# A hybrid decoder trunk on one NeuronCore: operand places in SBUF, the order of four stretches, and a latent projection in three passes

## What is computed

```python
def reference(x, p, positions, ...):
    for i in range(DEPTH):                       # DEPTH = 2
        proj = rms_norm(x, attn_norm[i]) @ w_in[i]     # stick-breaking, latent, window and block heads
        # A: z = q k^T / 8; log_beta = log_sigmoid(z); log_keep = log_sigmoid(-z), strictly causal
        #    tail = reversed cumulative sum of shifted log_keep; w = exp(log_beta + tail); o_a = w v
        # B: c_q, c_kv = rms_norm of 192 and 128 of proj's 352 latent columns, 32 more are the rotary key
        #    q, k, v from c_q @ mla_w_uq and c_kv @ mla_w_ukv; causal softmax
        # C: window of 128, 2 kv heads, sinks; D: block attention (one block here): causal softmax
        x = x + rms_norm(groups) @ w_o[i]              # the four groups side by side
        u = causal_depthwise_conv(rms_norm(x, ffn_norm[i]) @ w_up[i])     # 1024 -> 2 x 2816, width 3
        x = x + (silu(u[..., :2816]) * u[..., 2816:]) @ w_down[i]
        x = x + (p[i] @ ple_proj[i]) * sigmoid(x @ ple_gate[i])
    return x
```

## Time and profile before

| what | value |
|---|---|
| median of three runs | 682.27 us (681.94 to 682.47) |
| the profiled execution's own time | 682.88 us, its span 681.1 us |
| TensorE busy | 669.8 us, 98% of the span |
| VectorE, ScalarE, GpSimd busy | 438.0, 420.8 and 391.7 us |
| mean granted TensorE clock | 1.0 |
| DMA | 115.18 MB, 168 GB/s of HBM over the span |

### The profile page before, as it was taken

How to read it: one execution, slowest core, us unless ns; L and a number is a source line. 1 busy time by engine, 2 the same in 40 slices (tenths; PEclk the granted TensorE clock), 3 DMA queues, 4 the chain that set the end, 5 groups by cost and what they waited for, 6 DMA issues and landing times.

```text
span 681.1 us, 9499 instructions
## 1 busy us (share of the span) xinstructions
PE 669.8 (98%) x3772; PEld 578.2 (85%) x3772; DVE 438.0 (64%) x619; ACT 420.8 (62%) x627; POOL 391.7 (58%) x214
## 2 busy tenths in 40 slices
PE   7999999999999999999999999999999999999997
PEld 5988988888888888888889889888888888888885
DVE  6876877739898985003378587866589898920033
ACT  5559775667777775334464797646777767643342
POOL 5423200278888887987830232104888888889871
PEclk9999999999999999999999999999999999999999
DMA  9951132575565555553396422144555555555411
GB/s 321 384 199 63 63 109 78 185 242 187 186 191 192 194 192 197 201 193 104 105 305 210 136 83 92 63 146 164 187 188 191 192 192 194 192 204 193 155 31 63
DMA packets 74445, 115.18 MB, mean 169 GB/s; under 512 B 2336, under 2 KB 58272, under 8 KB 74144
## 3 DMA queue, kind: packets, MB, share of 16 engines
q1 hardware_dynamic: 73248, 111.75, 49.1%
q10 hardware_dynamic: 1152, 2.81, 1.1%
HBM read 113.51 MB, written 1.05 MB: 168 GB/s over the span
## 4 chain that ended last, share of the span: by engine, by line
PE 92%; ACT 3%; DVE 3%; DMA 1%; issue 0%; SPq 0%; ACTq 0%; DVEq 0%
PE ps L1356 23%; PE ps L924 13%; PE ps L926 13%; PE ps L925 13%; PE ps L1358 12%; PE ps L938 2%; PE ps L1011 2%; PE ps L1048 2%; PE ps L976 1%; PE ps L1031 1%; PE ps L1002 1%; DMA raw<-w_in 1%; PE ps L1041 1%; DVE wl L1547 1%; ACT pr L601 1%; PE ps L1133 1%
## 5 line engine op out<-in xcount | busy, mean ns | idle before, releaser
L453 POOL TENSOR_TENSOR wl<-raw,wh 128x2048 fp32r<-128x2048 f32 (+1 forms) x72 | 323.9, 4503 | 81.9 <-ACT wh L570 81.9
L1356 PE MATMUL ps<-hT_hl,wh 128*128 128x512 f32 x688 | 239.6, 392 | 0.0
L570 ACT ACTIVATE wh<-raw 128x2048 fp32r<-128x2048 f32 (+1 forms) x102 | 186.0, 1828 | 75.5 <-PE ps L926 69.4
L1358 PE MATMUL ps<-hT_hl,wl 128*128 128x256 f32 x688 | 193.7, 282 | 0.0
L1356 PEld LDWEIGHTS ps<-hT_hl,wh 128*128 128x128 f32 x688 | 129.2, 188 | 28.7
L1358 PEld LDWEIGHTS ps<-hT_hl,wl 128*128 128x128 f32 x688 | 129.4, 188 | 0.0
L440 POOL TENSOR_SCALAR st<-st 128x2 f32<-128x2 f32 (+3 forms) x26 | 8.1, 310 | 148.2 <-ACT lat L629 75.1
L924 PE MATMUL ps<-wh,hT_hl 128*128 128x512 f32 (+1 forms) x220 | 80.6, 366 | 0.0
L926 PE MATMUL ps<-wh,hT_hl 128*128 128x512 f32 (+1 forms) x220 | 79.1, 359 | 0.0
L925 PE MATMUL ps<-wl,hT_hl 128*128 128x512 f32 (+1 forms) x220 | 78.9, 358 | 0.0
L1831 DVE TENSOR_TENSOR x<-x,ps 128x512 f32<-128x512 f32 x16 | 10.8, 687 | 100.1 <-PE ps L926 98.0
(11 more groups left out here) (296 smaller groups left out, 1164.7 us busy)
## 6 DMA issues: line engine op xcount, KB each, us to landing
raw<-w_up SPq DMA_DIRECT2D x44, 1024.0 KB, 5.1
raw<-w_down SPq DMA_DIRECT2D x22, 1024.0 KB, 4.9
raw<-w_in SPq DMA_DIRECT2D x16, 1024.0 KB, 8.7
raw<-w_o SPq DMA_DIRECT2D x6, 1024.0 KB, 4.9
raw<-ple_gate SPq DMA_DIRECT2D x6, 1024.0 KB, 4.9
raw<-w_in SPq DMA_DIRECT2D x4, 704.0 KB, 5.3
ng<-norm_gains ACTq DMA_DIRECT2D x2, 1024.0 KB, 6.1
raw<-w_o SPq DMA_DIRECT2D x4, 512.0 KB, 3.5
```

Source lines behind the costliest of these rows:

```text
L453: pool.tensor_tensor(wl[:, slot, 0:n], raw[:, slot, 0:n], w_high(u)[:, 0:n].bitcast(F32), ALU.subtract).then_inc(ffn_l_made, 1)
L570: act.activation(w_high(u)[:, c:n], raw[:, slot, c:n], ACT.Copy).then_inc(h_made, 1)
L1356: pe.matmul(both, high[:, c], hU_all[:, k].rearrange("p a n -> p (a n)"), start=k == 0, stop=False, skip_group_check=True)
L1358: mm = pe.matmul(o, wl[:, slot, c], hU_h[:, k, :], start=False, stop=k == KT - 1, skip_group_check=True)
```

## The change

The changes are these. The slots of `wh` become three tensors with small tables between them, so that they start 9,216 bytes apart (8,320 before), and most other tensors are put in another order; the FFN still reads `wh` 128 bytes further on. `M_MLA_B` in layer 0 and `M_MLA_A`'s second token tile in layer 1 are multiplied in three passes, with new high and low parts (`latent_high`, `latent_low`, `latent_A`). The row of roots is made by two transposes. `high(3)` and `low(3)` stand ahead of the scaling and the sums of the latents. The softplus sums stand ahead of `mla_T(1)`, with `low(8)`, `high(8)` and the low parts `sp_low` moved in the same way. The transposes of the probabilities of groups 1 and 2 stand ahead of an output quarter. The first two `x_T` of layer 1 stand inside layer 0's last gate products.

```diff
-        wh = sb("wh", [P, RING, SLOT + UP_AT], F32R)
-        sb("wh_edge", [P, 256 - RING * UP_AT])
+        wh0 = sb("wh0", [P, SLOT + UP_AT], F32R)
+        rope_c = sb("rope_c", [P, TT, HD])
+        ident_b = sb("ident_b", [P, P], BF16)
+        inv_freq = sb("inv_freq", [P, HD // 2])
+        wh1 = sb("wh1", [P, SLOT + UP_AT], F32R)
+        rope_s = sb("rope_s", [P, TT, HD])
+        causal = sb("causal", [P, P], BF16)
+        gcol = sb("gcol", [P, DEPTH, KT])
+        neg_half = sb("neg_half", [P, 16])
+        wh2 = sb("wh2", [P, SLOT + UP_AT], F32R)
+        neg_tri = sb("neg_tri", [P, P])
+        above = sb("above", [P, P], BF16)
+        sb("wh_edge", [P, 32])
+        wh = (wh0, wh1, wh2)
         x = sb("x", [P, TT, D])
...
+        rope_c32 = sb("rope_c32", [P, TT, PE_DIM])
+        rope_s32 = sb("rope_s32", [P, TT, PE_DIM])
+        kpe = sb("kpe", [P, TT, PE_DIM])
+        sb("hT_edge", [P, 32])
...
+        with nc.sbuf_tensor("g_late", [P, 2, STEPS - EARLY, 2, SEQ], F32R) as g_late:
+            pass
+        hn = sb("hn", [P, TT, D])
+        lat = sb("lat", [P, 1280])
+        with nc.sbuf_tensor("mT_r", [P, 2 * H * SEQ], F32R) as mT_r:
+            pass
+        mT = sb("mT", [P, 2, H, SEQ])
+        v_moba = sb("v_moba", [P, TT, GW])
+        v_swa = sb("v_swa", [P, TT, 2 * HD])
...
-            return wh[:, u % RING, a:a + SLOT]
+            return wh[u % RING][:, a:a + SLOT]
...
+                def latent_high(a, unit, layer, name):
+
+                    n = COLS[unit]
+                    act.wait_ge(raw_landed[unit], (layer * (UNITS // DEEP) + 1) * 16)
+                    act.activation(a[:, 0:n], raw[:, unit, 0:n], ACT.Copy).then_inc(F[name], 1)
...
+                    latent_high(pt_r, M_MLA_B, 0, "mla_high")
...
                 act.dma_start(conv[:], conv_cols[layer]).then_inc(F["conv_landed"], 16)
+                high(3)
                 act.wait_ge(F["roots"], base["roots"] + 2)
                 for t in range(TT):
                     rooted(pr[:, 0, t, 0:MLA_COLS], ps[:, t, 0:MLA_COLS], t, "unit", M_MLA_B,
@@ -674,7 +687,6 @@
                     act.wait_ge(F["pr_ready"], base["pr_ready"] + t + 1)
                     act.activation(rot[:, t, 0:MLA_COLS], pr[:, 0, t, 0:MLA_COLS], ACT.Square
                                    ).then_inc(F["squared"], 1)
-                high(3)
                 act.wait_ge(F["uq_landed"], base["uq_landed"] + 16)
                 act.wait_ge(F["uq2_landed"], base["uq2_landed"] + 16)
...
                     act.wait_ge(F["sb_soft"], base["sb_soft"] + b + 1)
                     act.activation(sp_h[b], sb_sp[:, b * 512:(b + 1) * 512], ACT.Copy
                                    ).then_inc(F["sp_high"], 1)
+                high(8)
                 mT_out(0)
-                high(8)
                 high(9)
                 mT_out(1)
                 high(10)
...
+                    latent_high(pt_r, M_MLA_B, layer + 1, "mla_high")
+                    latent_high(pb_r, M_MLA_A, layer + 1, "mla_a_high")
...
+                def latent_A(t):
+
+                    tok = slice(t * P, (t + 1) * P)
+                    pe.wait_ge(F["mla_a_low"], layer)
+                    pe.wait_ge(F["xT_low"], base["xT_low"] + 2 * t + 1)
+                    for k in range(KT // 2):
+                        c = slice(k * MLA_COLS, (k + 1) * MLA_COLS)
+                        mm = split_product(ps[:, t, 0:MLA_COLS], hT_h[:, k, tok], hT_l[:, k, tok],
+                                           pb_r[:, c], mT_r[:, c], k == 0, False)
+                    mm.then_inc(w_used, 1)
+
...
                 if layer == 0:
                     x_T(x, AT_START, None)
                     project_tile(M_MLA_A, 0, (0, 1), 0, quarters=0)
                     project_tile(M_MLA_A, 1, (0, 1), 0, quarters=0)
-                    project_tile(M_MLA_B, 0, (0, 1), 0, quarters=1)
-                    project_tile(M_MLA_B, 1, (0, 1), 0, quarters=1)
+                    for t in range(TT):
+                        latent_B(t, False)
+                        latent_B(t, True)
                 else:
-                    x_T(x, AT_START, None, quarters=(0, 1))
+                    x_T(x, AT_START, None, quarters=(2,))
                     project_tile(M_MLA_A, 0, (0, 1), 0, quarters=0)
-                    x_T(x, AT_START, None, quarters=(2,))
                     latent_B(0, False)
                     x_T(x, AT_START, None, quarters=(3,))
                     latent_B(0, True)
-                    project_tile(M_MLA_A, 1, (0, 1), 0, quarters=0)
+                    latent_A(1)
                     latent_B(1, False)
                     latent_B(1, True)
                 pe.wait_ge(F["xT_low"], base["xT_low"] + 4)
                 pe.wait_ge(F["sbq_low"], base["sbq_low"] + 1)
                 project_T(M_SB_Q, 2, blocks=range(0, KT // 2), halves=True)
                 project_T(M_SB_Q, 2, blocks=range(KT // 2, KT))
-                pe.wait_ge(F["diag_made"], base["diag_made"] + 1)
-                pe.matmul(ps[:, 7, 256:512], neg_ones[:], tmp[:, 768:1024], start=True,
-                          stop=True, skip_group_check=True).then_inc(F["row_root"], 1)
+                pe.wait_ge(F["roots_wide"], base["roots_wide"] + 1)
+                for t in range(TT):
+                    mm = pe.transpose(ps[:, 7, 256 + t * P:256 + (t + 1) * P],
+                                      tmp[:, 768 + t * P:768 + (t + 1) * P], ident[:])
+                mm.then_inc(F["row_root"], 1)
                 project_T(M_SB_K, 3, columns=(0,))
...
                 pe.wait_ge(F["pr_ready"], base["pr_ready"] + 3)
                 project_tile(M_SWA_A, 1, SWA_BANKS, 0)
-                pe.wait_ge(F["mT_ready"], base["mT_ready"] + 2)
-                mla_T(1)
-
                 pe.wait_ge(signs_made, 2)
                 pe.wait_ge(F["sp_low"], base["sp_low"] + 3)
...
                 pe.matmul(ps[:, 6, :], neg_tri_r[:], pt_r[:, 1024:1536], start=False, stop=True,
                           skip_group_check=True).then_inc(F["sb_minus"], 1)
+                pe.wait_ge(F["mT_ready"], base["mT_ready"] + 2)
+                mla_T(1)
...
                 project_out(0, (2,))
                 group_T(1)
+                probs_T(1)
                 project_out(0, (3,))
-                probs_T(1)
                 pe.wait_ge(F["mix_low"], base["mix_low"] + 2)
                 pv(1, lambda h, k: v_moba[:, k, h * HD:(h + 1) * HD], 7)
                 scores(2, lambda h: qk_swa[:, h, :], lambda h: qk_swa[:, H, :], above, GROUPED)
                 project_out(1, (0, 1, 2))
                 group_T(2)
+                probs_T(2)
                 project_out(1, (3,))
-                probs_T(2)
                 pe.wait_ge(F["mix_low"], base["mix_low"] + 3)
                 pv(2, lambda h, k: v_swa[:, k, (h // 2) * HD:(h // 2 + 1) * HD], 7,
                    GROUPED)
...
                         mm = gate(n, 1, half)
                         if half == 1:
                             mm.then_inc(w_used, 1)
+                        if half == 1 and n == 2 and layer + 1 < DEPTH:
+                            x_T(x, AT_START, ("x_done", 0), quarters=(0, 1))
...
+                def latent_low(o, a, unit, n, high, low):
+
+                    dve.wait_ge(F[high], n)
+                    c = slice(0, COLS[unit])
+                    tt(o[:, c], raw[:, unit, c], a[:, c].bitcast(F32), ALU.subtract
+                       ).then_inc(F[low], 1)
+
...
                     x_low(0, AT_START)
+                    latent_low(wl[:, M_MLA_B], pt_r, M_MLA_B, 1, "mla_high", "mla_low")
...
-                    last = ts(tmp[:, 768 + t * P:768 + (t + 1) * P], ident[:],
+                    last = ts(tmp[:, 768 + t * P:768 + (t + 1) * P], neg_ones[:],
                               stat(ST_X + 6 + t), -1.0, ALU.mult, ALU.mult)
-                last.then_inc(F["diag_made"], 1)
+                last.then_inc(F["roots_wide"], 1)
                 if layer == 0:
                     rope_tables()
+                low(3)
...
                     c = slice(b * 512, (b + 1) * 512)
                     dve.wait_ge(F["sp_high"], base["sp_high"] + b + 1)
                     tt(pt_r[:, c], sb_sp[:, c], sp_h[b].bitcast(F32), ALU.subtract
                        ).then_inc(F["sp_low"], 1)
+                dve.wait_ge(F["squared"], base["squared"] + 6)
+                head_sums(ST_B, H, rot, 3)
                 low(8)
+                dve.wait_ge(F["tables"], base["tables"] + 1)
+                rotate(2, 0, H)
                 keys_scaled(ST_B, H, 5)
                 chained(rotate(3, GW, H))
...
+                    latent_low(wl[:, M_MLA_B], pt_r, M_MLA_B, layer + 2, "mla_high", "mla_low")
+                    latent_low(mT_r, pb_r, M_MLA_A, layer + 1, "mla_a_high", "mla_a_low")
```

70 lines of the change are left out of this document (19 added, 51 removed).

## The result

| | median | lowest to highest | runs |
|---|---|---|---|
| before | 682.27 us | 681.87 to 683.06 | 19 |
| changed | 683.00 us | 682.59 to 685.46 | 19 |

The ratio is 1.0015 (95% interval 1.0008 to 1.0022): 0.7 us slower, where 677.3 us was predicted with a range of 675.5 to 679.5. It lies within the 0.2% that was named as no change. First the page of the changed kernel: its span, TensorE's busy time and the chain, by engine and by line.

What follows compares the result with a forecast made beforehand. TensorE, 92% of the chain, was taken as the bound. The terms -0.8 - 0.85 - 0.9 - 0.9 + 0.2 - 1.7 = -4.95 took 682.88 us to 677.9, the median to 677.3, range 675.5 to 679.5.

Steps and rivals of the forecast that it cites:

- Part 3: Softplus sums ahead of mla_T(1): TensorE reaches the values' products earlier, limited by ScalarE's Exp, -0.45 us in each layer.
- Part 4: Output quarters behind the probabilities' transposes: no wait ahead of the values' products, -0.23 us four times, -0.9 us.
- Parts 1 and 2: Layer 0's latents in three passes, -0.8 us; row of roots by two transposes, low(3) earlier, -0.45 and -0.4 us.
- Part 5: Entry to layer 1, first transposes inside the last gate products: new waits against the three passes' saving, +0.2 us.
- Part 6: Places of wh's slots, 9,216 bytes apart: faster FFN, down, mixer and gate units, -1.7 us.
- rivals A and D: A: places change nothing, 679.0 us, chance 0.12; D: the common placement is the slow one, 684.5 us, chance 0.03.
- Rival C: New waits at M_SB_Q, x_done, low(8) and the probabilities eat most of the gain: -1.6, 680.6 us, chance 0.06.
- Rival B: More comes through, by earlier Exp, the entry's three passes and places: -6.7, 675.6 us, chance 0.07.
- The signs: Trace features named as proof, among them SB_Q near 17.3 to 17.5 us and about 0.5 us of wait for Exp.

Runs made afterwards that it cites:

- undo_sums_order: Changed kernel with the softplus sums, their subtractions, low(8) and high(8) back in the old order on TensorE, VectorE and ScalarE: 679.55 us, ratio 0.9948.
- heads_before_softplus: Changed kernel with only the heads' reduction moved ahead of the three softplus subtractions on VectorE: 679.88 us, ratio 0.9957.
- low8_behind_rotation: Changed kernel with only low(8) moved behind the second rotation on VectorE: 680.44 us, ratio 0.9961.
- part3_alone: Kernel before with only the softplus sums ahead of mla_T(1) and the moves of subtractions, low(8) and high(8) that belong to it: 686.42 us, ratio 1.0057.
- quarter2_ahead: Changed kernel with the last output quarter of group 2 ahead of the probabilities' transposes again: 682.22 us, ratio 0.9990.
- quarters_alone: Kernel before with only both last output quarters moved behind the probabilities' transposes: 683.37 us, ratio 1.0007.
- low14_behind_norm: Changed kernel with only low(14) moved behind the last group's division and norm on VectorE: 683.00 us, ratio 0.9999.
- places_alone: Kernel before with only the operand places of the changed kernel: 680.40 us, ratio 0.9968.
- reordered_latent_tile_fp32: Changed kernel with heads' sums ahead of subtractions, ScalarE's second mT copies behind Exp, low(14) behind last norm, and layer 1's second M_MLA_A tile float32 again: 676.13 us.
- old_sums_low14_behind: Changed kernel with the softplus sums' old order on all three engines and low(14) behind the last group's norm: 677.96 us, ratio 0.9929.

## Why the prediction was wrong

**Part 3 is the step that failed** (-0.9 forecast, +3.5 measured). The prediction followed the moved subtractions forward to TensorE's sums, and took ScalarE's Exp for "The next thing that TensorE needs". As far as the Exp it was right: the sums stand directly behind SWA_A, TensorE then waits 0.46 us for the Exp (about 0.5 forecast), and the products with the values start 24.64 us behind the scores where they stood 24.91 us behind them. That is a gain of 0.27 us there (0.45 forecast). It didn't follow what was queued behind the subtractions on VectorE. It saw that "the reductions and the first rotation stood between", and put the three in front of them without a price.

Behind that reduction stand GpSimd's roots, the scaled keys, a rotation, two low parts, the copy of group 1 and its norm: 22 us of work, some of it dependent and some only queued, with the 1.0 us of room named above (the section on the profile after). Counted from the scores, the reduction starts 2.3 us later than before (1.9 us of subtractions, and ScalarE's high part to wait for ahead of them). The mean takes 1.6 us more beside low(8), the root 0.3 more and the scaling behind them 1.4 less, so the scaled keys start 2.8 us later. The room takes 1.0 of that, and 1.7 arrived on TensorE in each layer. The lead won by then (2.1 us in the profiled execution) hid nothing, since the chain starts from TensorE's scores and moved with it. undo_sums_order, heads_before_softplus, low8_behind_rotation and part3_alone show this, from both kernels. The gain of part 3 was real but small: with the Exp no longer held by the second mT copy, it was 0.4 us a layer.

**Part 4** (-0.9 forecast, +0.7 measured). What it priced was right, each quarter gives its 0.23. Its bounds, "0 and -0.9", left out a loss, and that is where it lies: the quarter's last product frees a ring slot, and high(14), low(14) and the last group's division stand in that order behind it. quarter2_ahead, quarters_alone and low14_behind_norm agree in their stages.

**Parts 1 and 2** held. With TensorE at its full rate early, the stretch from the first float32 product to SB_Q is 9.30 us with float32 latents (places_alone) and 8.96 with three passes: -0.34, and -0.19 more because SB_Q's first product has no change of kind ahead of it (0.31 us to its first product with the low part, where it took 0.50), so about -0.5 (predicted -0.8; TensorE waited 0.35 us for the new low half). The roots gave -0.6 in each layer, more than the 0.45 and 0.4, as the wait for low(3) and the float32 pair both went:

```profile
22.59 0.38 PE L1118 MATMUL ps<-ident,tmp 128*128 128x128 f32 x2
22.73 0.36 PE L935 MATMUL ps<-hT_hl,wh 128*128 128x256 f32 x1
```

**Part 5** cost +0.3 beside the places' gain there (predicted +0.2). The wait ahead of the three-pass tile came with 0.83 us, as predicted. The sum took the three passes and this wait as even; by reordered_latent_tile_fp32 the float32 tile is 0.95 us better, so that the close total is partly luck. What else the two new operations on VectorE cost was not taken apart.

**Part 6** held: -1.9 (predicted -1.7), and rivals A and D are out. The Trainium skill, "SBUF — State Buffer", Who interferes with whom, gives TensorE read ports of its own and has it wait for no other engine. Taken as the prediction took it, places would then do nothing, and the trace of places_alone disagrees (5.55 us where 5.61 stood). Whether another engine has a part in it, and why an operand's place changes the step at all, is not settled here.

**The sum.** -0.5 - 1.2 + 3.5 + 0.7 + 0.3 - 1.9 = +0.9, measured +0.7. With parts 3 and 4 as forecast it would have been -5.1. Rival C named two of the places, "low(8) and the probabilities miss by a few tenths (+1.5)", but neither missed: TensorE waited for low(8) at SWA_B as little as for the probabilities. What these two moves cost lay elsewhere, at the roots and at the ring slot. Rival B's terms add up to -6.9, not -6.7, which changes nothing.

**The signs.** Most of what was named as proof came true: no wait behind the roots' transposes, the sums behind SWA_A and then about 0.5 us for the Exp, no gap ahead of the products with the values, 0.8 us ahead of the three-pass products, FFN units at 5.55. None of the signs looked at the transposes of the normed groups, where the time went.

## What to carry to other kernels

When an instruction is moved ahead of others on an engine, price what it now delays, each item to the place where TensorE next asks for it, with the room that is left there; 1.0 us of room doesn't take a delay of 2.8 us. When a product is moved that frees a buffer, the copy that waits for the buffer moves with it, and so does everything queued behind that copy. A lead won upstream doesn't cover a longer chain that starts downstream of it.

## What was not expected of the hardware

**After one wait TensorE ran at half its clock.** In low14_behind_norm, layer 1, TensorE stands still for 1.8 us ahead of group 1, starts again at 416.04, and the granted clock falls at about 416.3. The windows (busy time and count of PE, PEld, DVE, ACT, POOL, then the granted clock, the DMA share and GB/s):

```profile
414.00:415.00 1.00, 0.24 (x3) 0.04 (x1) 0.13 (x1) 1.00 (x5) 0.88 (x2) 1.00 0.00 0
415.00:416.00 1.00, 0.00 (x0) 0.00 (x0) 0.90 (x3) 0.84 (x4) 0.00 (x0) 1.00 0.00 0
416.00:417.00 1.00, 0.96 (x6) 0.97 (x7) 1.00 (x3) 0.11 (x1) 0.00 (x0) 0.70 0.00 0
417.00:418.00 1.00, 1.00 (x7) 1.00 (x6) 1.00 (x4) 0.98 (x3) 0.00 (x0) 0.50 0.07 16
...
420.00:421.00 1.00, 1.00 (x11) 1.00 (x10) 0.79 (x2) 1.00 (x1) 0.00 (x0) 1.00 0.00 0
```

For over 3 us the granted clock is 0.50, the level of 1.2 GHz, and the stage is 1.54 us longer than its twin in layer 0. The profiled executions hold eight such waits of 1.8 us (after, part3_alone, quarter2_ahead and low14_behind_norm, two layers each); the other seven left the clock alone. So such a wait cost 1.8 us seven times and about 3.3 once. That the wait is the cause is argued, not shown. Five of the six runs of the upper clump show a mean granted clock of 0.997, where the lower ones show 0.998 to 1.000.

**TensorE's first products run at half rate for a time that differs.** The same 16 float32 records of the latents, in the changed kernel and in old_sums_low14_behind:

```profile
7.80 5.00 PE L949 MATMUL ps<-raw,hT 128*128 128x352 f32 x16
```

```profile
8.47 7.19 PE L949 MATMUL ps<-raw,hT 128*128 128x352 f32 x16 [0.53 <-DMA raw<-w_in]
```

That is 0.31 and 0.45 us each; in the second one six of them step by 0.59 us, twice the usual 0.30, although both kernels are the same up to there. The granted clock of the records is 1.00 in both, so it doesn't show this. SB_Q starts anywhere from 16.70 to 19.36 us in the 14 profiled executions, which is more than parts 1 and 2 are worth; a difference there has to be read per stage. The Trainium skill, "TensorE: Matmul & The Clock Gate", Part 1, says that the number of slow first matmuls varies between runs of one kernel; these traces agree, with no slow step in undo_sums_order and seven in old_sums_low14_behind for the same opening code.

**GpSimd's mean waits for VectorE, its root doesn't.** The mean of the sums takes 0.20 us alone, 0.71 beside a rotation of 0.69, 1.22 when 1.2 us of low(14) are left, and 2.31 beside low(8)'s 2.29: each time it ends with VectorE's instruction. The 16-wide root behind it and VectorE don't hold each other so. In the kernel before low(8) starts in the root's last 0.7 us and takes its usual length:

```profile
60.63 2.95 POOL L445 TENSOR_TENSOR st<-st,neg_half 128x16 f32<-128x16 f32 x1
...
62.91 2.28 DVE L1547 TENSOR_TENSOR wl<-raw,wh 128x2048 fp32r<-128x2048 f32 x1
```

The Trainium skill, "SBUF — State Buffer", Who interferes with whom, which the prediction cites in part 5, has two such instructions contend; read as the prediction reads it, as an exclusion for a whole instruction, the mean agrees and the root doesn't.
